# Weight slots 32 bytes further apart, and the tiles behind them moved, in a two-block network on one core

## The reference

```python
for l in range(2):                                  # first block
    x = x + 0.5 * swiglu(rms_norm(x), wg1, wu1, wd1)        # d_ff 2816
    x = x + concat(attention(q, k, v), short_conv(...)) @ w_out
    x = x + 0.5 * swiglu(rms_norm(x), wg2, wu2, wd2)
x = rms_norm(x)
h = concat(meta_tokens, x)                          # second block, 272 tokens
proj = rms_norm(h) @ w_in                           # latents, gates, q, k, v
y = concat(mla(...) * silu(g_mla), neighbourhood(...) * silu(g_na))
out = (h + y @ w_out)[16:]
```

## Time and profile before

| | before |
|---|---|
| median of 3 runs | 1254.76 us (1251.52 to 1254.94) |
| the profiled execution | 1248.0 us |
| its span, first to last instruction | 1246.2 us |
| mean granted TensorE clock in it | 0.992 |
| TensorE matmul busy | 1210.2 us, 97% |
| VectorE busy | 820.1 us, 66% |
| ScalarE busy | 656.4 us, 53% |
| matmuls | 10050 |

### The profile page before, as it was taken

One profiled execution on the slowest core, in us unless ns is written; L12 is line 12 of the kernel. 1 busy time (PEld: TensorE's weight loads), 2 busy tenths in 40 slices (PEclk: granted clock), 3 DMA queues, 4 the chain that ended last, 5 costly groups with the idle time before them and its releaser, 6 DMA issues.

```text
span 1246.2 us, 27436 instructions
## 1 busy us (share of the span) xinstructions
PE 1210.2 (97%) x10050; PEld 1170.8 (94%) x10050; DVE 820.1 (66%) x1388; ACT 656.4 (53%) x1121; POOL 169.2 (14%) x228
## 2 busy tenths in 40 slices
PE   6999999999999999999999999999998999998998
PEld 6999999999999999999999999999996887998888
DVE  6777665867666655777655867767656666645764
ACT  5555543646444544555544546555445666646652
POOL 3000000351000000000010451000000000401960
PEclk9999999999999999999999999999997999999999
DMA  7655754445555654556754335556652430543542
GB/s 281 200 197 196 233 172 140 143 136 189 182 188 196 225 167 131 192 193 206 231 173 140 133 134 193 200 187 212 226 166 69 135 130 6 177 146 138 175 145 85
DMA packets 56742, 210.91 MB, mean 169 GB/s; under 512 B 7200, under 2 KB 9280, under 8 KB 56544
## 3 DMA queue, kind: packets, MB, share of 16 engines
q1 hardware_dynamic: 54048, 203.45, 49.0%
q0 software_dynamic: 2480, 6.48, 1.8%
q10 hardware_dynamic: 144, 0.06, 0.0%
HBM read 208.91 MB, written 1.05 MB: 168 GB/s over the span
## 4 chain that ended last, share of the span: by engine, by line
PE 92%; DVE 4%; ACT 2%; issue 2%; DMA 0%; DVEq 0%; ACTq 0%; SPq 0%
PE bank L1149 27%; PE bank L1151 26%; PE bank L1150 26%; PE bank L1187 2%; PE bank L1492 2%; DVE w_lo L735 1%; DVE h_lo L754 1%; PE bank L1472 1%; ACT w_hi L452 1%; PE bank L1457 1%; PE bank L1394 1%; PE bank L1396 1%; PE bank L1395 1%; PE bank L1452 1%; DVE h L748 1%
## 5 line engine op out<-in xcount | busy, mean ns | idle before, releaser
L1149 PE MATMUL bank<-h_hi,w_hi 128*128 128x256 f32 (+1 forms) x1992 | 565.8, 284 | 17.1 <-DVE w_lo L735 11.7
L1151 PE MATMUL bank<-h_hi,w_lo 128*128 128x256 f32 (+1 forms) x1992 | 556.1, 279 | 0.0
L1150 PE MATMUL bank<-h_lo,w_hi 128*128 128x256 f32 (+1 forms) x1992 | 555.9, 279 | 0.0
L735 DVE TENSOR_TENSOR w_lo<-w_raw,w_hi 128x1024 fp32r<-128x1024 f32 (+1 forms) x360 | 466.0, 1296 | 79.8 <-ACT w_hi L452 79.2
L452 ACT ACTIVATE w_hi<-w_raw 128x1024 fp32r<-128x1024 f32 (+1 forms) x360 | 397.7, 1108 | 91.4 <-PE bank L1151 69.3
L1149 PEld LDWEIGHTS bank<-h_hi,w_hi 128*128 128x128 f32 x1992 | 376.1, 189 | 25.9 <-issue 21.1
L1151 PEld LDWEIGHTS bank<-h_hi,w_lo 128*128 128x128 f32 x1992 | 378.6, 190 | 0.0
L1150 PEld LDWEIGHTS bank<-h_lo,w_hi 128*128 128x128 f32 x1992 | 376.3, 189 | 0.9
L1149 PE MATMUL bank<-g_hi,w_hi 128*128 128x256 f32 x832 | 231.4, 278 | 0.5 <-DVE x_res L920 0.5
L1151 PE MATMUL bank<-g_hi,w_lo 128*128 128x256 f32 x832 | 230.9, 278 | 0.0
L1150 PE MATMUL bank<-g_lo,w_hi 128*128 128x256 f32 x832 | 230.9, 278 | 0.0
(11 more groups left out here) (160 smaller groups left out, 1214.9 us busy)
## 6 DMA issues: line engine op xcount, KB each, us to landing
w_raw<-in_w SPq DMA_DIRECT2D x296, 512.0 KB, 3.3
w_raw<-in_wd SPq DMA_DIRECT2D x64, 704.0 KB, 4.1
w_raw<-in_relbias POOLq DMA_DIRECT2D x64, 64.0 KB, 2.3
btab_sb<-in_btab POOLq DMA_DIRECT2D x1, 1536.0 KB, 9.9
x_res<-in_xT SPq DMA_DIRECT2D x2, 512.0 KB, 4.9
out_T<-x_res SPq DMA_DIRECT2D x8, 128.0 KB, 1.7
rope_sb<-in_rope POOLq DMA_DIRECT2D x1, 272.0 KB, 3.5
mats_sb<-in_mats POOLq DMA_DIRECT2D x1, 192.0 KB, 3.7
```

The source lines that it names most:

```text
L735: dve.tensor_tensor(wlo[:, slot, 0:cols], raw[:, slot, 0:cols], whi[:, slot, 0:cols].bitcast(F32), ALU.subtract).then_inc(lo_ready[slot], 1)
L1149: pe.matmul(o, h, xh, start=first, stop=False)
L1150: pe.matmul(o, h, xl, start=False, stop=False)
L1151: return pe.matmul(o, lo, xh, start=False, stop=last)
```

## The change

`w_hi` and `w_lo` get slots of 1416 values instead of 1408, of which the last 8 are unused, so slot s begins 32*s bytes further on than before. An unused tile of 32 values is put between `w_hi` and `w_lo`. The unused tiles ahead of `h_hi` and `g_hi` grow from 48 to 56 and from 64 to 96 values. The one ahead of `y_hi` stays at 32. No instruction is added, removed or moved. All that differs is addresses.

```diff
         x = sb("x_res", [P, KT, TM])
         raw = sb("w_raw", [P, SLOTS, PTD])
-        whi = sb("w_hi", [P, SLOTS, PTD], F32R)
-        wlo = sb("w_lo", [P, SLOTS, PTD], F32R)
-
-        sb("h_hi_phase", [P, 48])
+        whi = sb("w_hi", [P, SLOTS, PTD + 8], F32R)
+        sb("w_lo_phase", [P, 32])
+        wlo = sb("w_lo", [P, SLOTS, PTD + 8], F32R)
+        sb("h_hi_phase", [P, 56])
         hhi = sb("h_hi", [P, KT * HS], F32R)
...
         with ExitStack() as first:
-            sb("g_hi_phase", [P, 64], F32, first)
+            sb("g_hi_phase", [P, 96], F32, first)
             ghi = sb("g_hi", [P, FT, T], F32R, first)
```

## The result

The changed kernel takes 1270.6 us (median of 4 runs, 1268.18 to 1271.73), the kernel before 1254.53 us. The ratio is 1.0152, 95% interval 1.0107 to 1.0197: slower. The profiled execution took 1271.73 us, its span 1269.9.

A forecast was written before the change was run, and what follows sets the result against it. The prediction took TensorE's matmul pitches to bound the kernel. To the profiled 1248.0 us it added 17.0 for h turning long, with g, y and the rest at 0, giving 1265.0 us, range 1234 to 1282.

The forecast's parts named there:

- The bound and the instrument: TensorE, 97% busy, bounds the kernel; addresses act only through matmul pitch, short or long by 4.44 ns, or by delaying another engine.
- all short: Every product of h, g and y at the short pitch: 14.1 us less, 1233.9 us; the slot-change rival's case, 25%.
- all long: Both h and g at the long pitch: 1248.0 + 17.0 + 7.4 = 1272.4 us.
- Slot 1: Matmuls reading h in slot 1, at distance 64, turn long as y's were; 4.3 us if this slot alone.
- I take long, since a pitch is kept from piece to piece: Slots 0, 2 and 3 of h follow slot 1 into the long pitch; h costs 17.0 us in all.
- this outcome: A sign of being wrong: pitch alternating from piece to piece with the slot, each distance having its own, no carry-over.
- The signs that I had named for being right: h_lo at a mean of 281 in every stretch, about 852 matmuls in 100 us of gate and up in both blocks.
- 17.0 us, all of it h: 1275 short products of h turn long at 13.3 ns each, added to the profiled 1248.0 us.
- g was to cost 0: Matmuls reading g stay as they are, 0 us; bounds +7.4 us if all long, -3.7 us if all short.
- That distances do nothing: Rival, 22%: pitch is drawn anew at each long interruption; time stays at the median 1254.8 us, 1247.8 to 1261.8.
- The 32-byte start: Rival, 15%: operands starting 32 bytes past a multiple of 64 need another step, short pitch 120.0 ns, 1291.6 us.
- a change of slot breaks the long pitch: Rival, 25%: the 32-byte step every 24 matmuls ends the long pitch, everything goes short, 1233.9 us.

## Why the prediction was right in its number and wrong in a step

**The bound and the instrument: right.** Only the pitch moved; the other engines' work and waits did not. The read of before as two pitches, 113.3 and 117.8 ns, each kept for a layer, was borne out by every trace with equal slots at 64 or 192, and so was the price of a layer (7.0 us): the bounds worked out from it, 1233.9 for all short and 1272.4 for all long, enclose all 23 runs of before on the first chip of the experiments, 1240.27 to 1267.72. That four of them lay within 1251.52 to 1254.94 was luck.

**Slot 1: wrong, and the wrong way round.** The step was "h, slot 1: distance 64, the one at which y is long throughout". From one tile at one distance in one execution I made a property of the distance. With h and g at 64 a whole layer was short, and in the changed kernel slot 1 is the only short slot of h in the layers (113.3 ns). What the rows showed was y after a break: pieces that stand alone, and the output projection behind them. For such pieces the reading mostly holds, for y at 64 in four traces and for slot 1 of h in the changed kernel (117.8 ns). It doesn't carry over to an unbroken stream of pieces in changing slots, where most of h runs.

**"I take long, since a pitch is kept from piece to piece": wrong.** In the changed kernel the pitch changes at each piece and is the same again in the next lap. With distances other than 64 and 192 among the slots it is kept only where the distance is kept. I had named this outcome among what would make the prediction wrong. The signs that I had named for being right appeared as well (h_lo at a mean of 281, 854 matmuls in 100 us for about 852), so they could not tell the two apart; the starts within one lap could.

**The terms.** Against the profiled execution of before the rise was to be 17.0 us, all of it h; it was 23.7, h in part and g. In the SwiGLU layers h cost 44 x 24 x (117.6 - 113.5) = 4.3 us in each of three, 12.9, less 0.3 in the layer that had been long. g was to cost 0; it cost 16 x 33 x (117.7 - 113.3) = 2.3 us in each of three, 6.9. The remainder, some 4 us, lies outside the SwiGLU layers. 119.9, 113.3, 116.7 and 120.0 have a mean of 117.5, so close to the long pitch of 117.8 that the total for h was near by luck. The total of 1270.6 lies between the forecast and 1272.4 (h and g long), mostly for the sake of g: the term that I had put at 0, with +7.4 us as its bound, came out at 6.9.

**The rivals.** That distances do nothing is refuted: 1283.51 us with nothing but two unused tiles resized. The Trainium skill says (page "TensorE: Matmul & The Clock Gate", section "Step-by-step: what each phase is for") that loading the next weights takes no bandwidth from the running matmul. What the prediction drew from it, that the distance could not matter, does not hold for this kernel's fp32r stream: up to 6.7 ns on top of 113.3 hang on where the two operands lie to each other. Whether bandwidth is what is lost no run shows. The 32-byte start is refuted by the kernel with all addresses 32 on. That a change of slot breaks the long pitch is true where both distances are among 64 and 192 (0.9931), but the changed kernel gives that up again with three bad distances in four.

**What stays open.** What the long pitch is, and what decides at a restart which one it will be. Why 160 runs at 117.3 ns in equal slots and at 120.1 behind a slot at 192. The changed kernel's own trace narrows this: its pieces of y in slot 2, also at 160 but after a break, run at 117.3, which points to the piece directly ahead. Why w_hi 192 with w_lo 64 stays short and its mirror does not. No run measured which reads meet in the memory; a conflict of the two reads is a guess, not something shown.

## What to carry to other kernels

Where the span is a row of matmuls that wait for nothing, measure the pitch from start to start, by stage, by buffer and within one lap of the slots, and apart for streams and for pieces that stand alone; a busy share of 97% hides 4% of difference. Then try the start of the stationary operand against that of the moving one modulo 256 bytes: here h and g at 192 from w_hi, with w_lo 128 bytes further on, gave 0.990 of the time for one more unused tile and a smaller one, and other distances up to 1.026. Before believing a difference of under 1% in such a kernel, take a dozen runs, since a layer can come out either way and is worth 7 us in 1250.

## What the runs showed of the hardware that I had not expected

- Two pitches for the same instructions at the same addresses, 113.3 and 117.8 ns for 256 fp32r columns at a granted clock of 1.00, each kept through up to 1584 matmuls in a row, and open to change only where the stream is interrupted.
- The pitch depends on the distance of the operands modulo 256 bytes, from 113.3 (64, 192) to 120.0 ns (0, 96), and not on their absolute place as far as one shift shows (all 32 bytes on: the same two pitches).
- A change of distance at a slot can end the long pitch within a piece (117.9, then 113.3 ns).
- The same slot at the same distance of 64 runs at 113.3 ns in a stream of pieces and at 117.8 ns after a break (changed kernel).
- With w_hi at 64 and w_lo at 192 the second pitch is 119.0 ns in place of 117.8.
